# Packed vectors, merged set-up, a PSUM bank for each first modulation unit, and one more split pair of down blocks on a ring of four

## The reference, cut to what matters

```python
for i in range(DEPTH):                       # DEPTH = 2
    mod = silu(c) @ w_mod[i] + b_mod[i]      # c: latent, c_ctx: context; 6 * D_MODEL columns
    h = rms_norm(x, g_pre1) * (1 + scale1) + shift1
    proj = h @ w_in                          # then conv + SSD scans | latent attention
    y = concat([y_ssd, o]) @ w_out           # y_ssd, o with norms ssd_norm, mla_norm
    x = x + gate1 * rms_norm(y, g_post1)
    h = rms_norm(x, g_pre2) * (1 + scale2) + shift2
    x = x + gate2 * rms_norm(ffn(h), g_post2)   # dense SwiGLU in layer 0, top-2-of-8 experts in layer 1

def expert(u, w_gate, w_up, w_down):         # widths 1024 -> 1408 -> 1024
    return (silu(u @ w_gate) * (u @ w_up)) @ w_down
```

## Time and profile before

| | |
|---|---|
| median of three runs | 2318.3 us |
| profiled execution | 2314.99 us, its span 2313.2 us |
| TensorE busy | 2010.6 us, 87% of the span |
| VectorE, ScalarE, GpSimd busy | 1280.2, 951.6 and 296.3 us |
| mean granted TensorE clock | 0.934 |
| data moved by DMA | 301.81 MB, 214200 packets, 52432 of them under 512 B |

### The profile page before, as it was taken

How to read it: one execution, slowest core, us unless ns; L and a number is a source line. 1 busy time by engine, 2 the same in 40 slices (tenths; PEclk the granted TensorE clock), 3 DMA queues, 4 the chain that set the end, 5 groups by cost and what they waited for, 6 DMA issues and landing times. The chain is left out here.

```text
span 2313.2 us, 33395 instructions
## 1 busy us (share of the span) xinstructions
PE 2010.6 (87%) x11887; PEld 1704.4 (74%) x11887; DVE 1280.2 (55%) x1956; ACT 951.6 (41%) x1514; POOL 296.3 (13%) x128
## 2 busy tenths in 40 slices
PE   2898699695999999995998699785899999999992
PEld 0897455495999999995996455685677788787881
DVE  1745667553222023205817667642688887778884
ACT  1414213424111111105214213430688887888872
POOL 0230000212333233320310000301000000000001
PEclk9899899897999999997999899895899999999996
DMA  7315503101222222201316700203996743727444
GB/s 193 104 42 182 181 18 110 59 16 55 74 81 80 59 74 73 85 26 37 86 30 228 273 3 1 73 1 137 382 410 237 277 191 144 304 77 290 182 154 191
DMA packets 214200, 301.81 MB, mean 130 GB/s; under 512 B 52432, under 2 KB 143312, under 8 KB 214096
## 3 DMA queue, kind: packets, MB, share of 16 engines
q1 hardware_dynamic: 187744, 279.28, 34.4%
q10 hardware_dynamic: 23472, 10.57, 1.7%
q0 software_dynamic: 2880, 10.49, 1.1%
HBM read 358.20 MB, written 28.61 MB: 167 GB/s over the span
## 5 line engine op out<-in xcount | busy, mean ns | idle before, releaser
L1919 DVE TENSOR_TENSOR ex_wl<-ex_raw,ex_wh 128x1024 fp32r<-128x1024 f32 x364 | 425.4, 1222 | 57.8 <-ACT ex_wh L1798 53.9
L1798 ACT ACTIVATE ex_wh<-ex_raw 128x1024 fp32r<-128x1024 f32 x364 | 370.7, 1057 | 39.6 <-PE psum L1856 35.5
L1856 PE MATMUL psum<-ex_wh,ex_he_hi 128*128 128x512 f32 (+1 forms) x624 | 242.6, 389 | 5.1 <-DVE ex_wl L1919 5.1
L1856 PE MATMUL psum<-ex_wl,ex_he_hi 128*128 128x512 f32 (+1 forms) x624 | 233.4, 374 | 0.0
L1856 PE MATMUL psum<-ex_wh,ex_he_lo 128*128 128x512 f32 (+1 forms) x624 | 233.1, 373 | 0.0
L2065 POOL TENSOR_TENSOR ex_wl<-ex_raw,ex_wh 128x1024 fp32r<-128x1024 f32 (+1 forms) x60 | 160.1, 2672 | 339.1 <-ACT ex_wh L2051 339.1
L2085 PE MATMUL psum<-h_hi,ex_wh 128*128 128x320 f32 x704 | 161.6, 311 | 17.6 <-POOL ex_wl L2065 15.3
L2051 ACT ACTIVATE ex_wh<-ex_raw 128x1024 fp32r<-128x1024 f32 (+1 forms) x60 | 68.4, 1142 | 258.7 <-PE psum L2085 244.4
L2085 PE MATMUL psum<-h_lo,ex_wh 128*128 128x320 f32 x704 | 161.2, 310 | 0.0
L2085 PE MATMUL psum<-h_hi,ex_wl 128*128 128x320 f32 x704 | 160.9, 310 | 0.0
L2113 DVE TENSOR_TENSOR ex_hf<-psum,ex_sg 128x640 f32<-128x640 f32 x22 | 18.1, 825 | 235.3 <-PE psum L2085 235.3
(11 more groups left out here) (377 smaller groups left out, 4361.0 us busy)
## 6 DMA issues: line engine op xcount, KB each, us to landing
ex_raw<-moe_gate_up SPq DMA_DIRECT2D x286, 512.0 KB
ex_raw<-moe_w_down SPq DMA_DIRECT2D x78, 512.0 KB
x<-moe_w_down SPq DMA_DIRECT2D x65, 512.0 KB
wmod_ssd<-w_mod SPq DMA_DIRECT2D x56, 512.0 KB, 5.7
wmod_at<-w_mod SPq DMA_DIRECT2D x24, 512.0 KB, 4.8
ex_raw<-ffn_w_gate SPq DMA_DIRECT2D x22, 512.0 KB, 3.8
ex_raw<-ffn_w_up SPq DMA_DIRECT2D x22, 512.0 KB, 3.9
ex_raw<-ffn_w_down SPq DMA_DIRECT2D x16, 704.0 KB, 4.6
```

What stands on the lines that cost most here:

```text
L1798: act.activation(wh[:, i % RING], raw_of(i), ACT.Copy).then_inc(*hi_done.up(1))
L1856: last = pe.matmul(p.psum[:, 2 + g % 2, 0:width], h[:, k], w[:, i % RING, cols], start=(k == 0 and m == 0), stop=(k == KD - 1 and m == 2))
L1919: dve.tensor_tensor(wl[:, i % RING], raw_of(i), wh[:, i % RING].bitcast(F32), ALU.subtract).then_inc(*lo_done.up(1))
```

## The change

- All small vectors (c, c_ctx, b_mod, the four gain vectors, conv taps and bias, q_norm, group norms) are packed on the host into one array of 128 rows with 270 values each and loaded by one DMA; the tiles become views of it. The loads at L301, L303, L512, L513, L1023, L1392 and L1393 and their waits go.
- `stage_setup` is merged into the first stage. ScalarE's queue issues the loads of x first.
- The four first modulation units use PSUM banks 0 to 3. `deviations` moves behind the second unit.
- `w_mod`, `w_in` and `w_out` are laid out on the host so that each load reads one contiguous run per partition (4 KB, 8 KB or more, 8 KB).
- SP waits for the cleared expert slots at the end of the second attention stage.
- In the experts `WHOLE_F` goes from 3 to 1 and `RING` from 5 to 4.

```diff
@@ Program.__init__
-        self.silu_c = sb("silu_c", [P, KD, 2])
+        self.vectors = sb("vectors_sb", [P, VECTOR_COLS])
+        self.silu_c = self.vectors[:, 0:2 * KD].rearrange("p (k s) -> p k s", k=KD)
...
@@ Modulation.on_tensor
+        bank = self.bank + n % self.banks
-        if kind == 0 and n >= 1:
-            pe.wait_ge(*self.taken.at(n))
+        if kind == 0 and n >= self.banks:
+            pe.wait_ge(*self.taken.at(n - self.banks + 1))
@@ stage_first_modulation
-        mod = Modulation(p, [(0, u) for u in range(2 * D // UNIT)], 0, own, "first", 8)
+        mod = Modulation(p, [(0, u) for u in range(2 * D // UNIT)], 0, own, "first", 8, banks=4)
             @block.sync
             def _(sp):
+                sp.dma_start(p.vectors[:], io["vectors"]).then_inc(*vectors_in.up(16))
                 mod.load(sp)
+            @block.gpsimd            # identity and masks, as in stage_setup
...
             @block.scalar
-                        act.dma_start(p.b_mod[:, l], io["b_mod"][l]...)        # and eight gain vectors
                 act.dma_start(p.x[:, 0:LB], ...)
                 act.dma_start(p.x[:, LB], ...)
+                act.wait_ge(*vectors_in.at(16))
+                act.activation(p.silu_c, p.silu_c, ACT.Silu).then_inc(*silu_done.up())
...
             @block.vector
-                dve.wait_ge(*small.at(160))
+                dve.wait_ge(*silu_done.at(1))
+                dve.tensor_copy(p.silu_wide[:, :, 0:2], p.silu_c).then_inc(*wide_ready.up())
                 for step in range(len(mod.steps)):
                     mod.on_vector(dve, step)
+                    if step == 2 * UNIT_STEPS - 1:
+                        deviations(p, dve, squared, mean, root)
                 mod.vectors(dve, link, 0, 0, ("scale",))
-                deviations(p, dve, squared, mean, root)
@@ stage_attention, SP
-                    sp.dma_start(gq[:], io["q_norm"][l]...).then_inc(*gains_in.up(16))
...
+                    sp.wait_ge(slots["cleared"], 16 * (MAX_BLOCKS + 1))
@@ stage_out_proj, SP
-                    sp.dma_start(gain[:, 0:4], io["ssd_norm"][l]...).then_inc(*small.up(16))
-                    sp.dma_start(gain[:, 4:8], io["mla_norm"][l]...).then_inc(*small.up(16))
                 for i in range(4):
                     if i >= 2:
                         sp.wait_ge(*lo_done.at(i - 1))
-                    sp.dma_start(raw[:, i % 2], io["w_out"][l, :, i * quarter:(i + 1) * quarter].rearrange(
-                        "(k p) f -> p k f", p=P)).then_inc(*landed[i % 2].up(16))
+                    sp.dma_start(raw[:, i % 2], io["w_out"][l, i].rearrange(
+                        "p (k f) -> p k f", k=KD)).then_inc(*landed[i % 2].up(16))
@@ stage_sparse_experts
-RING = 5
-WHOLE_F = 3
+RING = 4
+WHOLE_F = 1
-    credit = {lo_done: SPLIT, piece_done: N, hid: 2, whole_done: WG, ht_done: 1, x_turned: 1}
+    credit = {lo_done: SPLIT, piece_done: N, hid: 2, hl_done: 1, whole_done: WG, ht_done: 1, x_turned: 1}
@@ turn_hidden
-                            if g < 2:
-                                pe.wait_ge(*whole_done.at(b * WG + g + 1))
+                            if g == 1:
+                                pe.wait_ge(*whole_done.at(b * WG + 1))
                             else:
-                                pe.wait_ge(*hl_done.at(b * SPLIT_GROUPS + g - 1))
+                                pe.wait_ge(*hl_done.at(b * SPLIT_GROUPS + max(g - 1, 0) + 1))
@@ vector
+                            if i == GU + 5:
+                                low_hidden(SPLIT_GROUPS - 1)
```

More of the change, by code:

```diff
@@ L51 @@
 FAR = -1e30
+VECTORS = (("b_mod", NMOD * KD), ("gains", 4 * KD), ("conv_taps", XF * TAPS), ("conv_bias", XF), ("q_norm", QR // P),
+           ("group_norms", KD))
+LAYER_COLS = sum(n for _, n in VECTORS)
+VECTOR_COLS = 2 * KD + 2 * LAYER_COLS
 class Signal:
@@ L135, in chained @@
     return link
[L138 to L172, removed]
 UNIT = 512
@@ L186, with __init__ @@
 class Modulation:
-    def __init__(self, p, units, bank, own, tag, ring):
-        self.p, self.units, self.bank, self.ring = p, units, bank, ring
+    def __init__(self, p, units, bank, own, tag, ring, banks=1):
+        self.p, self.units, self.bank, self.banks, self.ring = p, units, bank, banks, ring
         if units:
@@ L230, in on_tensor @@
                 group = slice(32 * (QK * q + k), 32 * (QK * q + k + 1))
[L231 removed]
+                last = pe.matmul(p.psum[group, bank, :], p.silu_wide[:, (2 * kind + q) * QK + k, :],
                                  self.w[:, i % self.ring, k * UNIT:(k + 1) * UNIT],
@@ L509, in _ @@
             def _(sp):
-                with nc.allow_non_contiguous_dma(reason="small per-channel vectors"):
-                    for k in range(TAPS):
-                        sp.dma_start(cw[:, :, k], io["conv_w"][l, k].rearrange("(f p) -> p f", p=P)).then_inc(*small.up(16))
-                    sp.dma_start(cb[:], io["conv_b"][l].rearrange("(f p) -> p f", p=P)).then_inc(*small.up(16))
                 for i in pieces[2:]:
@@ L1021, in _ @@
             def _(sp):
-                with nc.allow_non_contiguous_dma(reason="one gain per partition"):
-                    sp.dma_start(gq[:], io["q_norm"][l].rearrange("(k p) -> p k", p=P)).then_inc(*gains_in.up(16))
                 sp.dma_start(kvrow[:], io["kv_norm"][l].partition_broadcast(P)).then_inc(*gains_in.up(16))
@@ L1363, in stage_out_proj @@
     nc, io = p.nc, p.io
-    landed, small = [p.sig(f"weights_landed{i}") for i in range(2)], p.sig("wo_small")
+    landed = [p.sig(f"weights_landed{i}") for i in range(2)]
     hi_done, lo_done, y_out = p.sig("weights_hi"), p.sig("weights_lo"), p.sig("yt_out")
@@ L1390, in _ @@
             def _(sp):
-                with nc.allow_non_contiguous_dma(reason="one gain per partition"):
-                    sp.dma_start(gain[:, 0:4], io["ssd_norm"][l].rearrange("(k p) -> p k", p=P)).then_inc(*small.up(16))
-                    sp.dma_start(gain[:, 4:8], io["mla_norm"][l].rearrange("(k p) -> p k", p=P)).then_inc(*small.up(16))
                 for i in range(4):
```

100 lines of the change are left out of this document (70 added, 30 removed).

## The result

The changed kernel takes 2291.48 us (median of 4 runs, 2283.91 to 2294.19), the kernel before 2317.78 in the same comparison: a ratio of 0.9879, 95% interval [0.985, 0.9909]. The forecast was 2293.5 with a range of 2282 to 2303. A second set of the changed kernel's runs gave 2291.41 (2290.59 to 2293.16). The profiled execution took 2294.19 us, span 2292.4, so it is the slowest of its four, 20.8 us under the profiled span of before; the medians are 26.3 apart. Each line is the change of one stretch's length, and a stretch ends where the next stage's first load goes out on SP's queue (in_proj: at its first product).

A forecast was written before the change was run, and what follows sets the result against it. Bounds: small loads then data at the start, TensorE's own work in the experts. Start -20.7, experts -9.1, attention -0.8, output projections +4.5 and +1.3 sum to -24.8 us: 2318.3 becomes 2293.5, range 2282 to 2303.

The forecast's parts named there:

- The start: First modulation stage: once small loads no longer hold it, data bound it and it ends 20.7 us earlier than 56.19.
- the forecast 31.7: Start: time in us when the last quarter of w_mod lands, 0.8 + 3.1 + 27.8 at 401 GB/s.
- The 0.4 us for slow steps: Start: allowance for TensorE waiting for data before each step, half the difference between steps of 1.94 and 1.06 us.
- Rival 2: Start: first load runs at 341 GB/s because w_mod alone sets the rate; 4.9 us less gain, 2298.4, chance 0.12.
- 0.4 was forecast: Attention: VectorE's chain starts 0.4 us earlier per layer without the q_norm issue ahead of sin, 0.8 us in all.
- 0.70 us a block: Experts: two down pieces a block become unsplit, 0.352 us less each, 9.1 us less over 13 blocks.
- Rivals 3 and 4: Experts: ring of four slips once a block, 2311.2, chance 0.03; or stalls TensorE every group of four, 2345, chance 0.02.
- +4.5: Output projection, layer 0: GpSimd's third low part goes ahead of y_lo, so TensorE starts 4.5 us later.
- +1.3: Output projection, layer 1: middle taken between TensorE starting 0.9 us earlier and y_lo shut out at +3.5 us.
- +3.5: Output projection, layer 1: cost in us if contiguous reads bring the third quarter over 3 us forward, shutting out y_lo.
- Rival 1: Output projections: nothing is lost, as VectorE goes first or the load doesn't come forward; sum -31.5, 2286.8, chance 0.22.

## Why the prediction was right, and where it was off

**The total: right in mechanism, and within 2 us partly by luck.** The two medians moved by 26.3 us, where 24.8 was forecast for the spans, but the two profiled spans moved by 20.8. By the table the start gave 1.5 us and pre-norm 1.6 more than forecast, the output projections cost 5.4 more, and the experts gave 1.1 less. The misses partly cancel, and the difference between medians and spans covers the rest.

**The start: right in mechanism, mis-sized by 1.5 us.** The data bound it. The rate was 419 GB/s instead of 401, which makes 11.15 MB 26.6 us instead of 27.8; the last step stood at 30.36, 1.3 us before the forecast 31.7. The 0.4 us for slow steps was not paid, as the last steps took 1.06 and 1.07 us. Of the parts, the order of the statistics with the banks is worth 1.85 us (undone alone), and w_mod's first load goes out 3.5 us earlier (1.24 instead of 4.71). The ten loads on ScalarE's queue cost 16.7 us when put back, but nearly all of that came by the SiLU, which they didn't hold up in the kernel before, so their share of the 22.2 stays unmeasured. Rival 2 took the 341 GB/s of the earlier trace rows for the rate of w_mod. That row has 2 KB pieces and small loads together. With 2 KB pieces alone the windows show 408, with small loads beside whole rows 403, and the changed kernel, with neither, 419. So it takes both to come down to 341, and why they do isn't shown.

**Pre-norm: 1.6 us that the forecast left out, and that aren't the change's.** In the first trace TensorE's first 64 products took 7.54 us instead of 9.17, and the granted clock over the stage was 0.86 of full speed, against 0.78 before. But the second trace of the same kernel has 9.17 us, 0.77 and a stage of 20.2, as before. Over all traces the stage takes either about 18.6 or 20.0 to 20.8 us. TensorE had been busy for 10.80 of the 16 us before the stage in the first trace, 10.09 in the second and 9.64 in the kernel before. That the one brings the other was not tested.

**The removed loads in attention: right, and small.** VectorE's chain began 4.27 us into the stage instead of 5.12 in layer 0 and 3.76 instead of 4.37 in layer 1, 0.85 and 0.61 us sooner where 0.4 was forecast. The input projections gained nothing, as forecast. The whole stretch of layer 1 is 0.5 us longer all the same, which no run here explains.

**The experts: right.** The forecast had 0.70 us a block, the traces show 0.63, or 8.2 us over 13 blocks; undoing that part alone gave 9.4 by the medians. In a new block four split down pieces took 5.54 and 5.47 us, the whole one 1.72, and the ring of four made TensorE wait nowhere within a block. At the tightest piece, the eighth, VectorE's row is this, in the block that begins at 1670.47:

```profile
1679.73 2.36 DVE L1900 TENSOR_TENSOR ex_wl<-ex_raw,ex_wh 128x1024 fp32r<-128x1024 f32 x2 [0.43 <-ACT ex_wh L1779]
```

It began 9.26 us into the block (9.3 forecast), so its first half was ready at about 10.4, and TensorE came to it at 10.9. That slack was enough. Rivals 3 and 4 fell.

**The output projection: the forecast collision came, and a second one with it.** Layer 0 was forecast at +4.5 and measured +5.2; layer 1 was forecast at +1.3 and measured +6.0 in one trace, +2.5 in the other. Two steps failed.

The first is the account of layer 0. It followed y_hi and y_lo and left out the first VectorE instruction of the stage that reads and writes SBUF, op_stat. In the kernel before, op_stat and GpSimd's first low part began in the same hundredth of a microsecond there (VectorE first), and so op_stat got away:

```profile
449.55 0.16 DVE L1478 TENSOR_SCALAR op_stat<-op_stat 128x10 f32<-128x10 f32 x1
449.55 4.53 POOL L1406 TENSOR_TENSOR op_w_lo<-mx_qkv_room,op_w_hi 128x2048 fp32r<-128x2048 f32 x1
451.32 0.22 DVE L1480 RECIPROCAL op_rstd<-op_rstd 128x10 f32<-128x10 f32 x1 [1.62 <-ACT op_rstd L1418]
```

The cast now comes 4.96 us after the stage's start instead of 6.69, and the race is lost. op_stat costs 3.7 us, y_lo 4.2, and an earlier start gives back 1.1: TensorE begins its products 6.8 us later in the stage, not 4.5. That the stage is still only 5.2 longer is luck for the sum. The rest of the stage took 91.6 us instead of 93.3, at a granted clock of 0.81 instead of 0.71 in the first products, so "TensorE starts later and the stage is longer by as much" didn't hold one to one.

The second is layer 1's +1.3, the middle between +3.5 (y_lo shut out) and a gain. The premise was a first quarter 1.0 us earlier; it landed 3.0 us sooner in the stage in the first trace and 2.3 in the second (GpSimd's cast at 5.58 and 6.24 us into the stage instead of 8.58). y_lo was shut out in both, so the end of +3.5 was the case. With op_stat getting away TensorE began 3.8 us later in the stage and the stage was 2.5 longer, and with op_stat caught too 7.5 later and 6.0 longer. In the kernel before, op_stat began 0.84 us before GpSimd's cast in layer 1 (1464.23 and 1465.07). Rival 1, nothing lost, fell too. The forecast's range had room for both outcomes.

Not every VectorE instruction is caught. The reciprocal above, on the same 128x10 values, took 0.22 us in the middle of a low part (449.55 to 454.08), and op_yf, which reads PSUM, took its usual 2.16 us beside one.

The prediction weighed the Trainium skill (SBUF — State Buffer, section Who interferes with whom), which describes an exclusive lock and says that issue order decides. The traces agree on the blocking: op_stat beside a low part took 3.89 and 4.36 us and ended with it, and beside the cast 1.20 us, again to its end. That section of the Trainium skill says as well that a tensor_scalar can take the shared pair when its operands meet conditions, which would have put op_stat on the list to look at. For the rate, the Trainium skill (DMA: Bandwidth & Descriptors, section Bandwidth) says that the memory side binds at about 358 GB/s, and the same section lists 425 GB/s for a 16 MB load with the pair's other core idle. The program ran on one core, and its 418 to 421 GB/s over 20 us agree with the second figure and not with the first.

**What stays open.** Why the dense stage is 1.1 us shorter and the router 1.1 longer. What the ten small loads cost without the SiLU behind them, and why 2 KB pieces and small loads together move only 341 to 348 GB/s. What the third buffer and the last low parts on VectorE are worth apart. And whether the fastest run of the changed kernel (2283.91) is one in which op_stat won in both layers: its spread of 10 us has the size of such races, but only two of its executions have a trace.

## What to carry to other kernels

A transfer that lands earlier releases an engine earlier, and what that engine then collides with has to be looked for among all instructions of its partner, the tiny ones at the head of a chain first: a lead of 0.63 us turned a 0.16 us instruction into one of 3.9. Work that two engines can't do side by side belongs on the one that does it faster and is idle there, here VectorE with 2.23 us against 4.5. When the first product comes earlier and the stage doesn't get shorter, look at the last buffer's chain (free, load, convert): with the first product at 17.3 us TensorE waited for the last low part, and the best version, which loads into a third buffer and has all low parts on VectorE, no longer waits there.

## What the runs showed of the hardware that was not expected

- A VectorE instruction on 128x10 values can wait for a whole GpSimd instruction on 128x2048: op_stat took 3.68 to 4.40 us beside a subtraction and 0.28 to 1.20 beside a cast, 0.16 alone. A reciprocal on the same values took 0.22 us in the middle of a subtraction.
- Ten loads of single values kept ScalarE's queue busy for 23.5 us ahead of x (0.79 to 24.29) and 28.6 us behind it (1.85 to 30.45), with nobody waiting for their data. The issue of the first gain load alone took 14.00 us in the one run and 19.55 in the other.
- The same program, on two executions, let VectorE or GpSimd go first, and the stage took 111.1 us in one and 107.6 in the other.
- 2 KB pieces with thousands of one-value descriptors beside them moved 341 to 348 GB/s (kernel before, 11 to 25 us); 2 KB pieces alone 408, whole rows beside the small loads 399 to 403 (8 to 14 us of the run with the small loads ahead of x).
